# The relative-position bias of one attention moved from VectorE's row maximum into TensorE's accumulation

## The reference

```
rel   = (LEFT_CHUNKS * CHUNK_2 + qi[:, None]) - kj[None, :]
bias  = rel_bias[:, jnp.clip(rel, -REL_CLIP, REL_CLIP) + REL_CLIP]
s     = einsum('bqhd,bkhd->bhqk', q, k) * scale + bias
s     = where(valid, s, NEG_INF)          # chunk-causal: 64-token chunks
p     = softmax(s);   o = p @ v
```

## Time and profile before

| what | value |
|---|---|
| three runs | 1239.43, 1240.6, 1243.27 us |
| profiled execution: its time / span in the profile | 1243.27 / 1241.5 us |
| PE busy | 1203.2 us (97%) |
| DVE, ACT, POOL busy | 580.6, 512.7, 454.9 us |
| DMA | 133.43 MB, mean 107 GB/s |
| scores of a=1, first to last | from 703.61 to about 735.4 us |
| values product of a=1 ends | about 746.7 us |

### The profile page before, as it was taken

The page is one execution under the profiler, slowest core; times in us unless marked ns, Lnnn a source line. Parts: engine busy times, 40 slices in busy tenths (PEclk is TensorE's granted clock), DMA queues, the critical chain, the costliest instruction groups (busy, mean ns, idle before and its releaser), DMA issues.

```text
span 1241.5 us, 16230 instructions
## 1 busy us (share of the span) xinstructions
PE 1203.2 (97%) x6022; PEld 971.7 (78%) x6022; DVE 580.6 (47%) x1084; ACT 512.7 (41%) x799; POOL 454.9 (37%) x158
## 2 busy tenths in 40 slices
PE   4999999999999999999999999899999999999998
PEld 4877767888888888888877665578888888888887
DVE  6444564777777774312540475753643433431000
ACT  5432453454334442332544478653544343332210
POOL 3443321353444443444453210113344433444442
PEclk9999989999999999999999999899999999999999
DMA  7233011355444552223332110011222222222322
GB/s 267 89 121 116 35 69 47 124 204 203 187 185 180 192 192 100 96 93 104 102 132 102 68 35 1 29 41 68 88 86 98 101 101 101 101 70 85 102 93 91
DMA packets 27634, 133.43 MB, mean 107 GB/s; under 512 B 3264, under 2 KB 6464, under 8 KB 18240
## 3 DMA queue, kind: packets, MB, share of 16 engines
q1 hardware_dynamic: 25696, 130.30, 29.3%
q10 hardware_dynamic: 1888, 2.47, 0.7%
HBM read 130.65 MB, written 2.10 MB: 107 GB/s over the span
## 4 chain that ended last, share of the span: by engine, by line
PE 82%; issue 10%; POOL 4%; DVE 3%; ACT 1%; DMA 0%; POOLq 0%; DVEq 0%; ACTq 0%
PE psum L1295 73%; POOL wl L426 2%; PE psum L1595 2%; PE psum L1709 2%; PE psum L1370 1%; PE psum L1380 1%; POOL wl L443 1%; PE psum L1654 1%; PE psum L1570 0%; DMA h<-xT 0%; DVE prob L1049 0%; ACT prob L602 0%; PE psum L1576 0%; DVE neg_max L1054 0%; PE psum L1535 0%
## 5 line engine op out<-in xcount | busy, mean ns | idle before, releaser
L426 POOL TENSOR_TENSOR wl<-raw,wh 128x2048 fp32r<-128x2048 f32 (+1 forms) x96 | 400.7, 4174 | 603.1 <-ACT wh L521 293.7
L1295 PE MATMUL psum<-xh,wh 128*128 128x512 f32 (+1 forms) x1088 | 412.9, 380 | 11.5 <-DVE xl L920 6.5
L1295 PE MATMUL psum<-xh,wl 128*128 128x512 f32 (+1 forms) x1088 | 405.8, 373 | 0.0
L1295 PE MATMUL psum<-xl,wh 128*128 128x512 f32 (+1 forms) x1088 | 405.7, 373 | 0.0
L1295 PEld LDWEIGHTS psum<-xh,wh 128*128 128x128 f32 x1088 | 206.0, 189 | 52.8 <-issue 9.1
L1295 PEld LDWEIGHTS psum<-xh,wl 128*128 128x128 f32 x1088 | 205.9, 189 | 36.1
L1295 PEld LDWEIGHTS psum<-xl,wh 128*128 128x128 f32 x1088 | 206.1, 189 | 35.7 <-issue 1.0
L997 DVE SCALAR_TENSOR_TENSOR scratch<-psum,cols,scratch 128x511 f32<-128x511 f32 (+1 forms) x176 | 131.6, 748 | 195.6 <-ACT scratch L658 187.3
L521 ACT ACTIVATE wh<-raw 128x2048 fp32r<-128x2048 f32 (+1 forms) x52 | 91.1, 1752 | 258.2 <-PE psum L1295 258.2
L1295 PE MATMUL psum<-acth,wh 128*128 128x512 f32 (+1 forms) x374 | 141.0, 377 | 0.0
L1295 PE MATMUL psum<-actl,wh 128*128 128x512 f32 (+1 forms) x374 | 140.8, 377 | 0.0
(11 more groups left out here) (220 smaller groups left out, 1282.7 us busy)
## 6 DMA issues: line engine op xcount, KB each, us to landing
raw<-stream SPq DMA_DIRECT2D x73, 1024.0 KB, 4.7
ada_raw<-ada SPq DMA_DIRECT2D x48, 512.0 KB, 5.5
raw<-down SPq DMA_DIRECT2D x32, 704.0 KB, 4.0
h<-xT SPq DMA_DIRECT2D x2, 1024.0 KB, 7.8
outT<-h SPq DMA_DIRECT2D x8, 256.0 KB, 5.1
rel<-rel_tiles ACTq DMA_DIRECT2D x1, 1344.0 KB, 9.8
wsT<-w_spatial_T SPq DMA_DIRECT2D x1, 512.0 KB, 10.0
k<-c_row SPq DMA_DIRECT2D x1, 512.0 KB, 10.6
```

The source lines that it names most:

```text
L426: pool.tensor_tensor(wl[slot][:, 0:w], raw[slot][:, 0:w], wh[slot][:, 0:w].bitcast(F32), ALU.subtract).then_inc(lo_done, 1)
L1295: ins = pe.matmul(out, lhs[a], rhs[b], start=first and n == 0, stop=last and n == 2)
```

## The change

The bias is added by PE. From the host comes one row of 640 numbers for each head (`rel_rows`). A DMA whose source steps by one element from partition to partition spreads it into a 128 x 512 tile, with the rows in reverse order. POOL splits the tile into a high and a low part in float32r (`rel_parts`), and PE adds both into the score banks with a reversed identity `flip_r` as the other operand (`relative`), which turns the rows the right way round. DVE then takes a plain row maximum, ACT reads PSUM, and PE waits for `att.exp` where it waited for `att.max`.

Tiles are now kept in rings: `rel` two, `rel_h` and `rel_l` four. Heads 0 and 1 are loaded where the table was, 2 and 3 just ahead of a=1, 4 and 5 in step 3, 6 and 7 in step 7. ACT issues two DMAs for each head.

```diff
-                rel = sb("rel", [P, HEADS, T], F32, s2)
+                rel = [sb(f"rel{b}", [P, T], F32, s2) for b in range(2)]
+                rel_h = [sb(f"rel_h{b}", [P, T], F32R, s2) for b in range(4)]
+                rel_l = [sb(f"rel_l{b}", [P, T], F32R, s2) for b in range(4)]
...
+            constant(pool.memset(flip[:, :], 0.0))
...
+            constant(pool.affine_select(out=flip[:, :], in_=flip[:, :], compare_op=ALU.not_equal, fill=1.0, base=1 - P,
+                               pattern=[[1, P]], channel_multiplier=1))
+            constant(pool.tensor_copy(flip_r[:, :], flip[:, :]))
...
-            constant(pool.memset(rel[0:64, :, T - 64:T], MASKED))
-            lows(base + 2, BASE2["mkv"])
+            for t in rel:
+                constant(pool.memset(t[64:P, T - 64:T], MASKED))
+            def rel_parts(hd):
+                source, high, low = rel[hd % 2], rel_h[hd % 4], rel_l[hd % 4]
+                pool.wait_ge(rel_landed[hd % 2], 32 * (hd // 2 + 1))
+                if hd >= 4:
+                    pool.wait_ge(att.qk, 2 * unit(1, TB * (hd // 2 - 1)))
+                pool.tensor_copy(high[:, :], source[:, :]).then_inc(rel_high, 1)
+                pool.wait_ge(rel_high, hd + 1)
+                pool.tensor_tensor(low[:, :], source[:, :], high[:, :].bitcast(F32), ALU.subtract).then_inc(rel_low, 1)
+            lows(base + 2, base + 4)
+            rel_parts(0)
+            rel_parts(1)
+            lows(base + 4, BASE2["mkv"])
+            for hd in range(2, HEADS):
+                rel_parts(hd)
             low_quarters(BASE2["mkv"], BASE2["out"] + 2)
...
-                            source, sign = (out, -1.0) if a == 1 else (scores_banks(a, V)[e][:, 0:w], 1.0)
-                            act.activation(out, source, ACT.Exp, bias=neg_max[:, c:c + 1],
-                                           scale=sign, accum_out=row_sum[:, c:c + 1]).then_inc(att.exp, 1)
+                            act.activation(prob[V % 4][:, e, 0:w], scores_banks(a, V)[e][:, 0:w], ACT.Exp, bias=neg_max[:, c:c + 1],
+                                           scale=1.0, accum_out=row_sum[:, c:c + 1]).then_inc(att.exp, 1)
...
+            def load_rel(hd):
+                if hd >= 2:
+                    act.wait_ge(rel_low, hd - 1)
+                src = bass.AP(rel_rows.tensor, hd * REL_LEN, [[1, P], [1, T - 64]])
+                act.dma_start(rel[hd % 2][:, 0:T - 64], src).then_inc(rel_landed[hd % 2], 16)
+                src = bass.AP(rel_rows.tensor, hd * REL_LEN + T - 64, [[1, 64], [1, 64]])
+                act.dma_start(rel[hd % 2][0:64, T - 64:T], src).then_inc(rel_landed[hd % 2], 16)
...
             split_next(base + 6, p2.mm, P2["v0"])
+            load_rel(2)
+            load_rel(3)
...
+                p, x = step // TB, step % TB
+                if x == 3 and p < 2:
+                    load_rel(2 * p + 4)
+                    load_rel(2 * p + 5)
...
-                        elif a == 1:
-                            dve.wait_ge(att.pt, V - 3)
-                            for e in range(2):
-                                dve.wait_ge(att.qk, 2 * V + e + 1)
-                                dve.tensor_tensor_reduce(prob[V % 4][:, e, 0:w], scores_banks(a, V)[e][:, 0:w], rel[:, 2 * (step // TB) + e, T - w:T],
-                                                         -1.0, FAR, ALU.add, ALU.min, neg_max[:, c + e:c + e + 1]).then_inc(att.max, 1)
...
-                            pe.wait_ge(att.max if a == 1 else att.exp, 2 * V - 2)
+                            pe.wait_ge(att.exp, 2 * V - 2)
...
+            def relative(p, i, e, out, w):
+                hd = 2 * p + e
+                if i == 0:
+                    pe.wait_ge(rel_low, hd + 1)
+                pe.matmul(out[:, 0:w], flip_r[:, :], rel_h[hd % 4][:, T - w:T], start=False, stop=False)
+                return pe.matmul(out[:, 0:w], flip_r[:, :], rel_l[hd % 4][:, T - w:T], start=False, stop=True)
```

More of the change, by code:

```diff
@@ L31 @@
 REL_CLIP = 128
+REL_LEN = T + P
 CHUNK = 2048
@@ L38 @@
 MASKED = -1e30
-FAR = 3e38
 H = T // 2
@@ L79, with build @@
     n_cols += count
[L82 removed]
+def build(nc, xT, cols_in, stream1, down1, stream2, down2, ada, c_row, w_spatial_T, b_spatial_rows, positions, rel_rows, outT):
     ctx = ExitStack()
@@ L181, in build @@
             ident_b2 = sb("ident_b2", [P, P], BF16, s)
+            flip = sb("flip", [P, P], F32, s)
+            flip_r = sb("flip_r", [P, P], F32R, s)
             ones96 = sb("ones96", [P, P], F32, s)
@@ L184, in build @@
             chunk_b = sb("chunk_b", [P, P], BF16, s)
-            sb("to_row2", [P, SMALL_PAD + 2 * P], F32, s)
+            sb("to_row2", [P, SMALL_PAD], F32, s)
             sq2 = [sb(f"sq2{b}", [P, T], F32, s) for b in range(2)]
@@ L205, in build @@
         rel_landed = [sem(f"rel_landed{b}") for b in range(2)]
+        rel_high, rel_low = sem("rel_high"), sem("rel_low")
         out_done = sem("out_done")
@@ L797, in _ @@
             act.wait_ge(res_down1.h, KD + 1)
-            load_rel(0, 0, 2)
-            load_rel(1, 2, HEADS)
+            load_rel(0)
+            load_rel(1)
             act.wait_ge(norm_final.ss, 1)
@@ L1254, in _ @@
                 dve.tensor_copy(v2[:, t, :], V2_BANKS[t][:, :]).then_inc(p2.dve, 1)
-            dve.wait_ge(setup2, 12)
-            dve.wait_ge(rel_landed[0], 32)
-            def rest_of_rel(step):
-                if step == TB:
-                    dve.wait_ge(rel_landed[1], 32)
-            attend(1, prob2, neg_max2, row_sum2, 0, rest_of_rel)
+            attend(1, prob2, neg_max2, row_sum2, 0)
             def mla_values(t):
@@ L1352, in attend @@
                         elif step >= 2:
-                            pe.wait_ge(att.max if a == 1 else att.exp, 2 * V - 2)
+                            pe.wait_ge(att.exp, 2 * V - 2)
                         for e in range(2):
-                            ins = scores(p, i, e, outs[e], w)
-                            if bias is None:
-                                ins.then_inc(att.qk, 1)
-                        if bias is not None:
-                            for e in range(2):
-                                bias(p, i, e, outs[e], w).then_inc(att.qk, 1)
+                            scores(p, i, e, outs[e], w)
+                        for e in range(2):
+                            bias(p, i, e, outs[e], w).then_inc(att.qk, 1)
                     if beside is not None:
@@ L1607, in _ @@
                 features_tile(bank[2 + e], (base + 1) % 2, e).then_inc(p2.mm, 1)
-            pe.wait_ge(setup2, 11)
+            pe.wait_ge(setup2, 14)
             def pair_sums(p):
@@ L1653, in chunked @@
             def chunked(p, i, e, out, w):
-                return pe.matmul(out[:, 0:w], cq[rows(e), p, P * i:P * i + P], ck[rows(e), p, 0:w], start=True, stop=True)
+                pe.matmul(out[:, 0:w], cq[rows(e), p, P * i:P * i + P], ck[rows(e), p, 0:w], start=True, stop=False)
+            def relative(p, i, e, out, w):
[4 more added lines that the diff above has]
+                return pe.matmul(out[:, 0:w], flip_r[:, :], rel_l[hd % 4][:, T - w:T], start=False, stop=True)
             nq, nk = BASE2["mq"], BASE2["mkv"]
@@ L1674, in first_heads @@
                     mla_head(step - STEPS - 1)
-            attend(1, chunked_ready, chunked, None, v2, prob2, probT2, ident2, first_heads)
+            attend(1, chunked_ready, chunked, relative, v2, prob2, probT2, ident2, first_heads)
             def mla_values(t):
@@ L1822 @@
     packed = np.concatenate([parts[name].astype(f32) for name in COLS], 1)
-    distance = np.clip(T - P + np.arange(P)[:, None] - np.arange(T)[None, :], -REL_CLIP, REL_CLIP)
+    distance = np.clip(T - 1 - np.arange(REL_LEN), -REL_CLIP, REL_CLIP)
     arrays = {
@@ L1837 @@
         "positions": f["positions_2"].reshape(1, T).astype(np.int32),
-        "rel_tiles": f["rel_bias_2"][0][:, distance + REL_CLIP].reshape(HEADS * P, T),
+        "rel_rows": f["rel_bias_2"][0][:, distance + REL_CLIP],
     }
```

5 lines of the change are left out of this document (removed).

## The result

Five paired runs gave 1249.21 us for the changed kernel (1248.43 to 1251.84) and 1242.79 for the kernel before (1239.43 to 1243.95): a ratio of 1.006 with an interval of 1.0041 to 1.0081. The change makes the kernel slower by 6.4 us by the medians, 7.5 by the ratio. The forecast was 11.3 us more and 1251.9 us in all, so the direction was right and the size half as large again as the ratio's 7.5. Both profiled executions: 1243.27 us before, 1250.6 after; spans 1241.5 and 1248.8. The kernel before has a run time that goes with its mean granted clock: in the comparison made last 20 of its 29 runs have 0.996 or more and a median of 1239.8 us, six have 0.990 to 0.993 and 1242.0 to 1244.3 us, and the profiled execution, at 0.990, is like these six.

A forecast was written before the change was run, and what follows sets the result against it. PE was taken to bound two thirds of the chunked attention. 11.4 (matmuls) + 0.2 (start-up) + 3.4 (DMA issues) - 3.7 (recovered) = 11.3 us more, 1251.9 us against the 1240.6 median; own range 1249 to 1254.5, wider range 1246.5 to 1257.5.

The forecast's parts named there:

- 64 matmuls, 11.4 us: PE in a=1: four added float32r matmuls in each of 16 steps, 9.8 us, plus 1.6 for changes of kind.
- Every load paid, 15.2 us: Rival on PE: every stationary operand's load is paid, 15.2 in place of 11.4 us, 1255.7 in all; chance 0.10.
- Start-up wait of the joint maximum, 0.2 us: At the start of a=1, older steps are missing to cover the chain of joint reduction and exponentials: 0.2 us added.
- ACT's DMA issues, 3.4 us: Issues in steps 3 and 7 delay ACT's copies, so PE stalls 2.2 and 1.2 us; bounds 0 and 4.8.
- Idle time and low clock recovered, 3.7 us: Early in a=1, added PE work fills 2.71 us of idle time and removes 1.0 us of low-clock loss.
- Tables late: Rival: tables of heads 6 and 7 are ready after 737, PE stops in step 12; 1255.5 us, chance 0.12.
- POOL holds DVE: Rival: eight more POOL instructions inside a=1 hold DVE 8 us, half seen at most: +4, 1256 us; chance 0.06.
- Added work vanishes: Rival: the stage is not PE's, idle time and low clock absorb the matmuls; +2.3, 1242.9 us; level has chance 0.05.
- a faster DVE shortens the chain: Rival: DVE's relief from the fused operations in a=1 brings more than the 3.7 us; faster has chance 0.01.

The follow-up runs named there:

- the two runs made from it: The kernel before with PE waiting for the exponentials in a=1, 1239.97 us; and the kernel before with its weight quarters in steps 6 to 9, 1240.28 us.

## Why the prediction was nearly right, and where it was wrong

- **64 matmuls, 11.4 us.** Measured 10.88, right within 5%. Pitches are 0.11, 0.12, 0.18 and 0.23 (taken 0.09, 0.12, 0.17, 0.23), and a change of kind costs 0.05 to 0.11 (taken 0.1). The four groups of pair 3 last 2.93 us with it, 11.7 for four pairs. The transposes behind them then start 0.2 us a pair sooner after one another, since a float32r matmul and not a float32 one stands ahead of them (from 735.40 to the product at 735.77 before, 742.72 to 743.02 after), which gives 0.8 back over the four pairs; I had not seen this.
- **Every load paid, 15.2 us.** Refuted. Matmuls one behind the other with the same row group and a load ahead of each have a pitch of 0.23 for 0.213 of columns; at 128 columns, where the load is longest against the stream, 0.11 for 0.05. The sentence of the Trainium skill ("TensorE: Matmul & The Clock Gate", The mechanism) that loads overlap only across row groups does not describe this trace at 512 columns. The same section also allows a load into a background weight buffer to be pulled ahead, which the trace does not speak against. At 128 columns a limit of the loads is not excluded.
- **Start-up wait of the joint maximum, 0.2 us.** Too small: 1.1 by the run with split maxima.
- **ACT's DMA issues, 3.4 us.** The step that failed. I added durations of issues to the chain of ACT's arithmetic as though the two shared one line. The trace has the issues beside running exponentials, with 0.26 and 0.75 us of ACT's idle time left, and the stalls of PE are 0.27 and 0.14 us where 2.2 and 1.2 were forecast; the run with the loads on SP measures 0.42 for both. The places were right, the overlap was not: without the bias matmuls the copies of steps 5 and 9 hold PE, for 1.4 us in all.
- **Idle time and low clock recovered, 3.7 us.** Measured 2.2 (10.88 - 8.67): PE's idle time ahead of the tail fell from 2.7 to 1.1. The other 0.6 us is what the low clock's loss leaves after the issues' 0.4 and short waits that the modelled ends of matmuls hide; I can't split it further. That loss was 1.3 us and not 1.0, since scores of 256 columns took longer too, as these lines of the kernel before show. (The wait of 0.43 us, which the prediction puts in step 6, stands in step 5.) Of the 1.1 left, 0.97 is waits for exponentials that the split maximum removed, so this term and the one on the start-up wait are one error.

```profile
710.48 1.05 PE L1654 MATMUL psum<-ck,cq 64*128 64x256 f32 x4
...
720.83 0.70 PE L1654 MATMUL psum<-ck,cq 64*128 64x256 f32 x4
```

- **The low clock was counted as the kernel's to recover.** No profile shows the kernel before with a full clock in its stage, so whether the stretch of 0.85 comes in each of its executions is not shown; its run times of the last comparison, and the stage's clock of 1.00 in the two runs made from it, say that it need not. At an equal mean clock of 0.996 or more the changed kernel has 1249.0 us (4 runs) and the kernel before 1239.8, so the change costs 9.2 us, as the stages say (53.20 - 44.05). The 7.5 of the ratio is less, since by their times three of the five runs it was paired with had the lower clock. By the later medians of before, 1239.97 to 1240.83, it would be 8.4 to 9.2. What sets the clock of an execution was not found.
- **Tables late.** Refuted: no wait of L1679 or L1680. The casts took 0.61 us, not 0.9, and the loads landed in 3.0 us (median). Heads 6 and 7 were ready at 727.2 and 729.1, wanted at 733.22.
- **POOL holds DVE.** Seen (1.35 for 0.35 us), and by the Trainium skill ("SBUF — State Buffer", Who interferes with whom) expected, but PE did not wait for it in the changed kernel. Its price in the prediction rests on a misread column: the earlier trace rows has DVE busy for 28.99 of 34.14 us, so 5 us were free and not 15 (15 is what PEld's 19.27 leaves). In the changed kernel 14 us were free, 27.41 busy of 41.86, since the stretch grew. Without the bias matmuls the tables' work on POOL costs 1.0 us, with the loads on SP.
- **Added work vanishes; a faster DVE shortens the chain.** Refuted as causes: PE is gapless in the last stretch and nearly so in the third. DVE's relief, together with exponentials that read PSUM, is worth 0.5 us once everything else is away.

So the forecast of 11.3 was 2.6 us above the stage's 8.7: 3.4 for the issues (the 0.4 that they cost is within the time not recovered), 0.5 for the matmuls and 0.2 for the start-up wait, less 1.5 for time not recovered (3.7 against 2.2). Two errors of opposite sign lie in it, so part of the nearness is luck. The total of 1249.21 us lies just inside the forecast's own range, and that range was reckoned from a median of 1240.6 where the paired runs have 1242.79. Against a kernel before at full clock it was 2.1 too high.

## What to carry to other kernels

Work that is moved to the engine without gaps costs its full length wherever that engine has no gap, and how much its own waits give back is read stretch by stretch, not from the stage's mean. Eight DMA issues on ACT, 3.7 us of them, added 1.0 us to ACT's arithmetic here and 0.4 to PE's path: ask whether the queue can run ahead, and whether PE has other work while it can't. Before idle time or a low clock is counted as something to be had, see whether other executions of the same kernel show it. And when work is moved to another queue, look at what else moves with it: here POOL's quarters came 5 us sooner.

## What the runs showed of the hardware that was not expected

- ACT's queue began two DMA issues, of 0.33 and 0.47 us, during a 0.69 us exponential that stands ahead of them in the program. Four issues, 1.9 us, left 0.26 and 0.75 us of idle time ahead of the next copy in the changed kernel, and 0.54 and 1.18 in the one without bias matmuls and with split maxima.
- A float32r matmul of 128 columns one behind the other has a pitch of 0.11 us, one of 256 columns 0.12: under 256 columns there was next to nothing to save.
- POOL's cast of 128 x 512 from float32 to float32r takes 0.61 us, half of its subtraction (1.27 to 1.33).
